# A two-block transformer kernel on one core: attention masks of block 1 added by accumulating transfers instead of VectorE, and modulation steps placed elsewhere

## The reference, cut to what matters

```python
# first_block
h = swiglu(rmsnorm(x, g), w_gate, w_up, w_down);  x = x + 0.5 * rmsnorm(h, g_post)
qkv = rmsnorm(x, mix_pre_g) @ w_qkv
# 8 heads, neighbourhood:  s = where(col_valid, q k^T * scale + rel_bias[...], -1e30)
# 8 heads, dilated mixture of three windows: s + t5_bias[bucket], masked, three softmaxes mixed by their log-sums
x = x + rmsnorm(concat(o_na, o_dil) @ w_out, g);  then swiglu again

# second_block, each layer l
m = silu(cond) @ w_mod[l] + b_mod[l]        # "modulation": 6 * 1024 values for each of c and c_ctx
```

## Time and profile before

| what | value |
|---|---|
| median of 3 runs | 1959.04 us (1958.63 to 1959.83) |
| the profiled execution | 1961.84 us |
| its span | 1959.9 us |
| TensorE busy in the span | 1907.1 us, 97% |
| VectorE busy | 1226.1 us, 63% |
| moved by DMA | 297.44 MB, 5 queues |

### The profile page before, as it was taken

The page is one execution under the profiler, slowest core; times in us unless marked ns, Lnnn a source line. Parts: engine busy times, 40 slices in busy tenths (PEclk is TensorE's granted clock), DMA queues, the critical chain, the costliest instruction groups (busy, mean ns, idle before and its releaser), DMA issues.

```text
span 1959.9 us, 31179 instructions
## 1 busy us (share of the span) xinstructions
PE 1907.1 (97%) x12606; PEld 1690.0 (86%) x12606; DVE 1226.1 (63%) x1951; ACT 947.5 (48%) x1511; POOL 475.5 (24%) x328
## 2 busy tenths in 40 slices
PE   8999999999999999999999999999999899899999
PEld 8999988999988888787788888888888898799988
DVE  5888898779856933646663742454377756685410
ACT  5444546655456443326643531243275454755643
POOL 2211022000000000003343354455400000304887
PEclk9999999999999999999999999999999999899999
DMA  8987664466833112211233354466432343164554
GB/s 292 276 261 264 196 207 164 149 224 233 273 123 100 63 55 97 87 43 44 76 108 108 119 172 149 161 215 206 150 108 98 108 140 97 44 194 140 183 194 151
DMA packets 83951, 297.44 MB, mean 152 GB/s; under 512 B 9704, under 2 KB 12912, under 8 KB 83424
## 3 DMA queue, kind: packets, MB, share of 16 engines
q1 hardware_dynamic: 65600, 232.81, 36.1%
q0 software_dynamic: 16592, 59.11, 9.6%
q10 hardware_dynamic: 1616, 3.52, 0.5%
HBM read 294.34 MB, written 2.54 MB: 151 GB/s over the span
## 4 chain that ended last, share of the span: by engine, by line
PE 80%; DVE 10%; ACT 4%; issue 3%; DMA 2%; POOL 0%; DVEq 0%; SPq 0%; ACTq 0%; POOLq 0%
PE ps L588 20%; PE ps L583 20%; PE ps L586 20%; DVE wl L451 3%; PE ps L580 3%; ACT wh L435 2%; DMA wr<-wstream 1%; PE ps L582 1%; PE ps L1361 1%; PE ps L1257 1%; PE ps L1262 1%; PE ps L1259 1%; PE ps L1401 1%; PE ps L1380 1%; PE ps L2089 1%
## 5 line engine op out<-in xcount | busy, mean ns | idle before, releaser
L583 PE MATMUL ps<-HH,wh 128*128 128x256 f32 (+1 forms) x2160 | 706.3, 327 | 2.3 <-ACT wh L435 1.4
L588 PE MATMUL ps<-HH,wl 128*128 128x256 f32 (+1 forms) x2160 | 692.7, 321 | 8.6 <-DVE wl L451 6.3
L586 PE MATMUL ps<-HL,wh 128*128 128x256 f32 (+1 forms) x2160 | 690.0, 319 | 0.0
L435 ACT ACTIVATE wh<-wr 128x1024 fp32r<-128x1024 f32 x440 | 459.1, 1052 | 338.8 <-PE ps L588 241.9
L451 DVE TENSOR_TENSOR wl<-wr,wh 128x1024 fp32r<-128x1024 f32 x301 | 367.0, 1223 | 202.6 <-ACT wh L435 201.4
L588 PEld LDWEIGHTS ps<-HH,wl 128*128 128x128 f32 x2160 | 412.5, 191 | 41.6 <-DVE wl L451 10.2
L583 PEld LDWEIGHTS ps<-HH,wh 128*128 128x128 f32 x2160 | 412.8, 191 | 38.6 <-issue 7.0
L586 PEld LDWEIGHTS ps<-HL,wh 128*128 128x128 f32 x2160 | 412.8, 191 | 30.9 <-issue 2.4
L451 POOL TENSOR_TENSOR wl<-wr,wh 128x1024 fp32r<-128x1024 f32 x139 | 337.8, 2433 | 221.9 <-ACT wh L435 220.5
L1516 POOL TENSOR_TENSOR s<-s,ST 128x512 f32<-128x512 f32 x56 | 57.3, 1040 | 674.8 <-DVE ST L1484 674.5
L1115 DVE CUSTOM_DVE_ANT_0 PROD<-WM,COND 128x1024 f32<-128x1024 f32 x104 | 127.5, 1239 | 1.3
(11 more groups left out here) (309 smaller groups left out, 3001.7 us busy)
## 6 DMA issues: line engine op xcount, KB each, us to landing
wr<-wstream SPq DMA_DIRECT2D x440, 512.0 KB, 3.7
WM<-wmod POOLq DMA_DIRECT2D x68, 512.0 KB, 3.9
X<-wmod POOLq DMA_DIRECT2D x28, 512.0 KB, 5.6
NAB<-naskew POOLq DMA_DIRECT2D x16, 128.0 KB, 6.6
DILB<-dilskew POOLq DMA_DIRECT2D x8, 256.0 KB, 7.9
COND<-cond ACTq DMA_DIRECT2D x2, 1024.0 KB, 4.7
CT<-consts POOLq DMA_DIRECT2D x1, 1216.0 KB, 7.8
X<-xin SPq DMA_DIRECT2D x4, 256.0 KB, 5.9
```

The source lines that it names most:

```text
L435: ins = e.activation(self.WH[i % NSPL][:, :], self.WR[n % NRAW][:, :], ACT.Copy)
L583: e.matmul(out, wh, xh, start=i == 0, stop=False)
L586: e.matmul(out, wh, xl, start=False, stop=False)
L588: return e.matmul(out, wl, xh, start=False, stop=i == n_k - 1)
```

## The change

`B1M` and its load go, and so do VectorE's four additions. In their place GpSimd issues four transfers with an accumulate: the mask is read from DRAM, each row of 256 values repeated for the 8 heads, and added to the table in SBUF. The two for `NAB` stand behind chunk 5 and ahead of the line's store; GpSimd first waits until all 16 loads of `NAB` have landed. The two for `DILB` stand behind chunk 10 and ahead of chunk 11; GpSimd first waits for the 8 loads of `DILB`. Attention now waits for the four transfers.

`FFN_MODS` still holds 22 steps, but slices 12 and 13 now have 1 and 2 in place of none, slices 8, 15, 18 and 20 have 1 in place of 2, and slice 19 has 2 in place of 1. The 18 side calls of the down projection are now all modulation steps (16 before), so all 56 are done by the end of the first value projection, and none is left for the output projection.

```diff
-FFN_MODS = [0, 0, 0, 0, 0, 1, 1, 2, 2, 1, 2, 1, 0, 0, 1, 2, 2, 1, 2, 1, 2, 1]
+FFN_MODS = [0, 0, 0, 0, 0, 1, 1, 2, 1, 1, 2, 1, 1, 2, 1, 1, 2, 1, 1, 2, 1, 1]
@@ pool_bias_loads
-        e.dma_start(self.B1M[:, :], self.d_bm).then_inc(L["bmask"], 16)
@@
             else:
                 self.pool_mod(e, w, 0, 0, n - 2)
+        self.pool_mask(e, w, self.NAB, 0, "nabias", 16)
         w.wait_ge(*self.c("skew").at("line"))
         e.dma_start(self.d_line, self.LNT[0:8, :]).then_inc(L["line"], 16)
@@
             self.pool_mod(e, w, 0, 0, 7 + b)
+        self.pool_mask(e, w, self.DILB, 1, "dilbias", 8)
         for ch in range(11, MOD_A):
             self.pool_mod(e, w, 0, 0, ch)
+
+    def pool_mask(self, e, w, table, m, load, n):
+        w.wait_ge(self.loads[load], 16 * n)
+        for a in range(2):
+            src = bass.AP(self.d_bm.tensor, 512 * m + 256 * a, [[1024, 128], [0, 8], [1, 256]])
+            e.dma_start(table[:, a], src, accum_op=ALU.add).then_inc(self.loads["bmask"], 16)
@@
-    def dve_bias_masks(self, e, w):
-        L = self.loads
-        w.wait_ge(L["bmask"], 16)
-        for m, B, ld, n in ((0, self.NAB, "nabias", 16), (1, self.DILB, "dilbias", 8)):
-            w.wait_ge(L[ld], 16 * n)
-            for a in range(2):
-                mk = self.B1M[:, 512 * m + 256 * a:512 * m + 256 * a + 256]
-                e.tensor_tensor(B[:, a], B[:, a], bc(mk, 1, 8), ALU.add).then_inc(*self.c("bias").mark((m, a)))
-                yield
@@ b1_free
-        return [self.c("bias").at((1, 1)), (self.loads["line"], 16), self.c("skew").at("levels")]
+        return [(self.loads["bmask"], 64), (self.loads["line"], 16), self.c("skew").at("levels")]
@@ dve
-        masks, setup = self.dve_bias_masks(e, w), self.dve_setup(e, w)
-        for f in self.dve_ffn(e, w, 1, "n1", [], itertools.chain(masks, mod), setup):
+        setup = self.dve_setup(e, w)
+        for f in self.dve_ffn(e, w, 1, "n1", [], mod, setup):
             if f == 7:
                 self.dve_bias_line(e, w)
-            if f in (12, 13):
-                next(masks)
             for _ in range(FFN_MODS[f]):
                 next(mod)
```

More of the change, by code:

```diff
@@ L223 @@
     "hi", "lo_dve", "lo_pool", "dense",
-    "set_v", "set_a", "skew", "bias", "mask",
+    "set_v", "set_a", "skew",
     "n_sq", "n_mm", "n_ln", "n_root", "n_v", "n_e2", "rt", "h_hi", "h_lo", "sq", "sq_sum", "resid",
@@ L342, in __init__ @@
         self.Y = at_("Y", 76, [8, 256])
-        self.B1M, self.OHT, self.T5T = at_("B1M", 84, [1024]), at_("OHT", 88, [512]), at_("T5T", 90, [8])
+        self.OHT, self.T5T = at_("OHT", 88, [512]), at_("T5T", 90, [8])
         self.LNT, self.LMF = at_("LNT", 91, [512]), at_("LMF", 93, [384])
```

## The result

| | before | changed |
|---|---|---|
| median | 1959.43 us (1958.63 to 1960.47, 4 runs) | 1977.5 us (1975.18 to 1979.36, 4 runs) |
| ratio | | 1.0092, 95% interval 1.0077 to 1.0107 |
| profiled execution, its span | 1961.84 us, 1959.9 us | 1978.1 us, 1976.2 us |
| VectorE busy | 1226.1 us | 1220.8 us |
| moved by DMA | 297.44 MB | 301.11 MB |

The change costs 18.1 us of the median. VectorE no longer makes its 9.2 us of additions, though its busy time falls by only 5.3 us (its products `PROD<-WM,COND` of block 2 took 2.1 us more, among others), and nothing came of what it won. The bytes rise by 3.67 MB, which is four times 1.05 MB less the mask's own load of 0.52 MB.

The account below looks back on a forecast made before the run. TensorE, nearly without gaps, was taken to bound the kernel, DMA engines second; episodes of 13.5 and 6.5 us less 2 gave +18, 1961.84 to 1979.8 profiled, median 1977, own range 1970 to 1984, overall 1959 to 1988.

Parts of the forecast that it names:

- The mechanism: On q0 the additions hold back chunks 6 and 11; VectorE stops for them and TensorE runs dry behind it.
- The total: Whole kernel: +18 us, profiled execution 1979.8, median 1977; chance 0.40 for 1970 to 1984.
- First episode: NAB's additions ahead of chunk 6, wanted at slice 14: VectorE loses 15 us, TensorE 13.5.
- Second episode: DILB's additions ahead of chunk 11, start of down projection: VectorE 6 us, TensorE 5, plus 1.5 for weights, 6.5 in all.
- The price: A pair's additions on q0 take 16 us of all 16 DMA engines, the second fetch counting as a second copy.
- When TensorE ran dry: First episode: TensorE stops 1.3 us after VectorE stops at 103; weights stop at 106 and q0 has the engines alone.
- The weights: Second episode: weights get 40% of the engines or less for 25 us, come 1.8 MB short, adding 1.5 us.
- Credits: 2 us subtracted from the sum, for gaps won and for the crowding at 110 to 130 us.
- The crowding of 110 to 130 us: The first stop spreads out the DMA crowding there; counted with the gaps won in the 2 us subtracted.
- The 1 us at the down projection: At its start two additions of 2.29 us give way to steps of 1.22 us; at most 1 us credited.
- After 180 us: From 180 us on, TensorE's gaps are those of the kernel before.

Follow-up runs that it names:

- kernel 1: The changed kernel with the four mask transfers left out, attention waiting for the table loads instead; 1957.05 us, ratio 0.9991 to the kernel before.
- 4: The changed kernel with NAB's pair moved behind chunk 21 and DILB's behind chunk 27, with its own semaphore; 1958.1 us, ratio 0.9987 to the kernel before.
- 10: The changed kernel with both pairs late, behind chunks 21 and 27, the same program measured a second time; 1956.26 us, ratio 0.9978 to the kernel before.
- kernel 6: The changed kernel with only DILB's pair moved behind chunk 27, NAB's pair staying early; 1966.81 us, ratio 1.0038 to the kernel before.
- 7: The changed kernel with only NAB's pair moved behind chunk 21, DILB's pair staying early; 1966.14 us, ratio 1.0040 to the kernel before.
- Kernel 5: The changed kernel with 26 more products of constants on TensorE ahead of slice 16's gate; 1977.36 us, ratio 1.0092 to the kernel before.
- kernel 2: The changed kernel with the four transfers as plain copies in the same places, without the addition; 1963.6 us, ratio 1.0023 to the kernel before.
- kernels 3: The changed kernel with VectorE's modulation steps at their old places, none at slices 12 and 13; 1973.79 us, ratio 1.0071 to the kernel before.

## Why the prediction was right, point by point

**The mechanism** held: the order on q0, chunk 6 late, chunk 11 late, the low halves of TensorE late behind them. Kernels 1, 4 and 10 show that the four transfers and their place are the whole loss, 6 and 7 that there are two stops.

**The total** (+18, measured +18.1) is nearer than the reasoning earned. At attention the loss was 20.4 us. By the trace it is made up of two holes of 12.5 and 7.4 us (forecast 13.5 and 5), the lower clock behind them, some 2.9 and 1.2 us (forecast: nothing), and no starved weights (forecast 1.5), less about 3.6 us that came back (forecast 2). Errors on both sides cancelled. The medians then differ by 2.3 us less than attention does; in the profiled pair the granted clock in block 2 took back 3.8 us, which the forecast did not have either.

**First episode.** Forecast: 15 us for VectorE, 13.5 for TensorE, line landed at 112. Measured: 13.8, 12.5, and 109.7.

**Second episode.** Forecast: wanted 164.5, landed 170.5, 6 us and 5. Measured: wanted 162.8, landed 170.9, 8.1 us and 7.4.

**The price** was mis-sized: 7.6 us of the engines for a MB, taken as two full copies, where the runs show 6.2 beside the weights and 6.3 with fewer of them. 16 us for a pair should have been 13. In the first episode this shows: the skewed copy and chunk 6 were out at 111.3 and not at 113.5. Chunk 6 then took 5.2 us and not 4.5, and the stop was 1.2 us shorter than forecast. In the second, the additions began late. Chunk 10 stood ahead of them on q0 (issued at 142.84, landed after 5.3 us), and from 143 to 148 us only 4 packets of their size moved:

```profile
DMA packets 359, 1.31 MB, mean 263 GB/s; under 512 B 38, under 2 KB 42, under 8 KB 358
```

So they ran from about 148 us, not 144, and were 3 us of the engines shorter than forecast; chunk 11 landed at 170.9, near the forecast's 170.5, by luck.

**When TensorE ran dry** was read wrongly. The forecast had it 1.3 us behind VectorE's stop, with the weights stopped at 106 and the additions alone on the engines from there. TensorE ran dry at 106.7, 4.1 us behind VectorE's stop at 102.6, and from 105 to 107 us the weights still had 78.9% of the engines and the whole of q0 29.8%. The loss of TensorE is all the same 1.3 us less than VectorE's (12.5 against 13.8), because after the landing VectorE needs 2.8 us (116.44 to 119.20) before TensorE can go on.

**The weights** were to come 1.8 MB short, and 1.5 us was added for it. They moved 1.64 to 1.91 MB in 10 us, and this term did not exist.

**The clock** was left out. It fell behind both holes, and slice 16 took 8.65 us (119.06 to 127.71) instead of 5.76. Kernel 5 bears on what that is worth: without the first fall the same time is lost to weights and chunk 11.

**Credits.** The crowding of 110 to 130 us won back 3.5 us (kernel 6), where I had put the whole of the credits at 2. The 1 us at the down projection can't be told apart: kernel 1 leaves 0 to 0.2% for all the edits that remove or move work on VectorE.

**After 180 us** next to nothing changed, as forecast: 20.4 us late at attention.

The rule of the Trainium skill that a transfer which adds reads two sources and so runs at about half the rate of a copy (Collectives: The Full Stack, The bandwidth ceiling; its measured ratio is 1.93, for the reduce step of a collective) gives the direction that this case bears out. What ratio this case has depends on the copy that is taken: 1.65 (6.2 against 3.8) or 1.7 (against kernel 2's 3.6) beside the weights, and 2.1 against the plain packets of 1 KB on q10. With the weights idle, from 112 to 118 us of the changed kernel, q0's plain transfers took 75.4% of 6 us for 1.38 MB, which is 3.3 us for a MB, and the ratio to 6.3 is 1.9:

```profile
q0 software_dynamic: 378, 1.38, 75.4%
```

So no run here contradicts the 1.93, and none shows that the second read is the reason.

## What to carry to other kernels

A transfer put into a queue costs the wait of what stands behind it, whatever it replaces: count the time until the next load in that queue is wanted, and put the transfer where that is longer than its landing, or where nothing follows. Here the same four additions cost 18 us in one place and nothing that the runs can tell in another. And a stop that ends with a landing absorbs some of what was won ahead of it: kernels 3 and 5 won 7 and 3.6 us at slice 14 and 16, and kept 4.6 and 1.0. A difference of 0.1 to 0.2% in the total is not yet a gain of the edit: look at whether it stands in the stage that was edited, and at the granted clock of the runs.

## What the hardware did that I had not expected

- An accumulating transfer of fp32 into SBUF took 6.2 to 6.3 us of the 16 engines for a MB, and moved in packets of 1 KB (996 for 1.00 MB). A plain copy by the same access pattern took 3.6 and moved in packets of 4 KB (433 for 1.70 MB, kernel 2). Its issue on GpSimd took 1.6 us (3.22 for two), that of the plain copy 0.9 us (1.77 for two, kernel 2).
- The weights queue kept its rate beside it: 1.70 MB from 85 to 95 us, where it had 1.29 MB beside kernel 2's plain copies.
- The granted clock fell about 5 us after TensorE ran dry (106.7 to 111), and came back 6 us after it had work again.
